# First gather ahead of the result rows, turns in place of unread products, and GpSimd making a quarter of two low parts of every item

## The reference, cut to what matters

```
logits = h @ w_router + b_router
top_val, top_idx = lax.top_k(logits, 4)
gates = softmax(top_val)
# for each expert e, over the tokens that chose it (their order is by expert):
hgu   = xs @ w_gate_up[e] + b_gate_up[e]          # 1024 -> 2048, gate and linear columns interleaved
act   = min(g,7) * sigmoid(1.702*min(g,7)) * (clip(l,-7,7) + 1)
out   = (act @ w_down[e] + b_down[e]) * gate      # 1024 -> 1024
moe   = segment_sum(out, token)
h     = layernorm(alpha * h + moe, ln2_g, ln2_b)
```

## Time and profile before

| | us |
|---|---|
| median of 3 runs | 1944.49 (1944.4 to 1946.3) |
| the profiled execution, whole | 1945.81 |
| its span | 1944.1 |
| ahead of the experts | about 690 |
| items 0 and 1 | about 757 to 830 |
| the loop of small and big items | about 830 to 1800 |
| three late items, final layernorm | about 1800 to 1944 |

### The profile page before, as it was taken

How to read it: one execution, slowest core, us unless ns; L and a number is a source line. 1 busy time by engine, 2 the same in 40 slices (tenths; PEclk the granted TensorE clock), 3 DMA queues, 4 the chain that set the end, 5 groups by cost and what they waited for, 6 DMA issues and landing times.

```text
span 1944.1 us, 28693 instructions
## 1 busy us (share of the span) xinstructions
PE 1849.6 (95%) x8487; PEld 1445.6 (74%) x8487; DVE 1665.5 (86%) x1783; ACT 1351.0 (69%) x1777; POOL 497.5 (26%) x395
## 2 busy tenths in 40 slices
PE   6999999998989997999999999999999999999887
PEld 3657767787768886877877787777778777777665
DVE  6899997448775566999999999999999999999887
ACT  4556865214346524798889888888888888888775
POOL 6671000000000114422421522423232322222121
PEclk7999999999999996999999999999999999999998
DMA  8222216332110157999999999999999999999994
GB/s 318 87 108 87 86 63 209 120 103 63 64 44 23 32 141 273 316 404 384 395 392 395 389 397 397 385 391 400 347 401 402 395 384 383 397 394 343 326 339 193
DMA packets 133073, 523.37 MB, mean 269 GB/s; under 512 B 15145, under 2 KB 20425, under 8 KB 112848
## 3 DMA queue, kind: packets, MB, share of 16 engines
q1 hardware_dynamic: 118704, 492.45, 66.5%
q0 software_dynamic: 14304, 30.11, 5.7%
HBM read 512.76 MB, written 19.29 MB: 274 GB/s over the span
## 4 chain that ended last, share of the span: by engine, by line
PE 39%; ACT 6%; DMA 6%; DVE 5%; issue 4%; ACTq 0%; SPq 0%; DVEq 0%
PE ps L1148 32%; DMA arena<-in_w_gate_up 6%; PE ps L1197 3%; DVE split L2851 3%; ACT arena_r L2046 2%; ACT split L2046 2%; ACT arena L2075 2%; PE ps L1101 1%; DVE arena_r L2851 1%; PE ps L1187 1%; DMA ring<-in_w_down 1%; DVE arena L2989 0%; DVE small L2982 0%; DVE aTs L2795 0%; SPq L675 0%
## 5 line engine op out<-in xcount | busy, mean ns | idle before, releaser
L1148 PE MATMUL ps<-split,xTs 128*128 128x512 f32 x2016 | 503.1, 397 | 8.4 <-DVE split L2851 5.4
L1148 PEld LDWEIGHTS ps<-split,xTs 128*128 128x128 f32 x2016 | 377.8, 190 | 103.8 <-DVE split L2851 19.3
L2851 DVE TENSOR_TENSOR split<-arena,split 128x2048 fp32r<-128x2048 f32 x166 | 376.9, 2284 | 11.5 <-ACT split L2046 10.6
L2046 ACT ACTIVATE split<-arena 128x1024 fp32r<-128x1024 f32 x332 | 330.1, 1052 | 28.6 <-DMA arena<-in_w_gate_up 19.2
L2851 DVE TENSOR_TENSOR split<-ring,split 128x2048 fp32r<-128x2048 f32 x106 | 241.5, 2292 | 0.0
L854 POOL DMA_INDIRECT y_rows<-arena,slots x33 | 144.8, 4389 | 305.4 <-issue 263.4
L2046 ACT ACTIVATE split<-ring 128x1024 fp32r<-128x1024 f32 x212 | 212.4, 1057 | 3.6 <-DMA ring<-in_w_gate_up 2.9
L2851 DVE TENSOR_TENSOR arena_r<-arena,arena_r 128x2048 fp32r<-128x2048 f32 x83 | 189.8, 2286 | 2.1 <-ACT arena_r L2046 2.1
L1148 PE MATMUL ps<-arena_r,xTs 128*128 128x512 f32 x672 | 180.7, 403 | 1.8 <-DVE arena_r L2851 1.6
L2046 ACT ACTIVATE arena_r<-arena 128x1024 fp32r<-128x1024 f32 x166 | 172.0, 1057 | 13.3 <-DMA arena<-in_w_gate_up 10.8
L1148 PE MATMUL ps<-arena_r,aTs 128*128 128x512 f32 x672 | 169.3, 397 | 0.0
(11 more groups left out here) (484 smaller groups left out, 3155.3 us busy)
## 6 DMA issues: line engine op xcount, KB each, us to landing
arena<-in_w_gate_up SPq DMA_DIRECT2D x170, 1024.0 KB, 13.8
ring<-in_w_gate_up SPq DMA_DIRECT2D x102, 1024.0 KB, 14.4
arena<-in_w_down SPq DMA_DIRECT2D x79, 1024.0 KB, 13.9
ring<-in_w_down SPq DMA_DIRECT2D x57, 1024.0 KB, 14.3
ring<-in_w_in SPq DMA_DIRECT2D x23, 1024.0 KB, 4.9
ring<-in_w_out SPq DMA_DIRECT2D x8, 1024.0 KB, 5.0
ring<-in_mod_w SPq DMA_DIRECT2D x10, 512.0 KB, 9.1
ring<-in_mod_w SPq DMA_DIRECT2D x4, 1024.0 KB, 4.9
```

The source lines that it names most:

```text
L1148: m = mm(ps[:, banks + q, :], lhs[:, x_, k, :], w[:, q * 512:(q + 1) * 512], start=start, stop=stop)
L2046: A(split_part(0, c), chunk(it, c), ACT.Copy).then_inc(sig("hi_ready"), 1)
L2851: V.tensor_tensor(split_pair(1, p), slot_tile(it.slot(p)), split_pair(0, p), ALU.subtract).then_inc(sig("lo_ready"), 1)
```

## The change

Five edits.

1. GpSimd gathers item 0's tokens ahead of the four `y_dram` stores, which now stand right behind that gather. The two loads of layernorm constants move behind the 16 stores of pairs, just ahead of item 1's rows.
2. SP loads item 0's tiles in the order `FIRST_LOADS`: 7 and 6 ahead of 3, 4 and 5, each at an earlier condition of its own.
3. The two bias loads count on one semaphore instead of two.
4. In small items `keep_busy(4)` is gone, and `turn_next` stands in its place, ahead of the second `turn_sum`.
5. In every item but item 0, GpSimd writes the first 512 of the 2048 columns of the low parts of pairs 6 and 8 (`pool_low`), and DVE the other 1536. PE waits for both before the low products of these pairs, ACT before it overwrites their high parts, SP before it reloads their slots. In GpSimd's order the first piece stands behind the `slot_g` load and the second behind the `slot_s` load.

The rest of the diff, cut to its core:

```
+FIRST_LOADS = (0, 1, 2, 7, 6, 3, 4, 5, 8, 9, 10, 11)
+POOL_PAIRS = (6, 8)
+POOL_WIDE = 512
+    def by_pool(self, p):
+        return self.i * len(POOL_PAIRS) + (POOL_PAIRS.index(p) + 1 - len(POOL_PAIRS))
...
-            for j in range(EXPERT_TILES):
+            for j in FIRST_LOADS:
                 if j < RING1:
                     sp.wait_ge(*last_use(max(n for n in range(N_PHASE1) if n % RING1 == j)))
+                elif j == RING1 + 4:
+                    sp.wait_ge(sig("bgu_lo"), 1)
+                elif j == RING1 + 3:
+                    sp.wait_ge(sig("o_used"), TC + 1)
                 elif j == RING1:
                     sp.wait_ge(sig("o_used"), TC + 2)
-                elif j == RING1 + 3:
-                    sp.wait_ge(sig("bgu_lo"), 1)
...
                 wait_alone(sp, sig("lo_ready"), sp.to_reg(it.pairs + (LEAD + j + 1)))
+                if it.pairs_shared and j in POOL_PAIRS:
+                    wait_alone(sp, sig("lo_pool"), sp.to_reg(it.by_pool(j)))
...
+            def pool_low(it, p):
+                c_ = slice(0, POOL_WIDE)
+                wait_alone(pool, sig("hi_ready"), pool.to_reg(it.pairs * 2 + (2 * p + 1)))
+                wait_alone(pool, sig("lo_used"), pool.to_reg(it.pairs + (p + 1)))
+                nc.gpsimd.tensor_tensor(split_pair(1, p)[:, c_], slot_tile(it.slot(p))[:, c_], split_pair(0, p)[:, c_], ALU.subtract).then_inc(sig("lo_pool"), 1)
...
                         pe.wait_ge(sig("lo_ready"), it.pairs + (LEAD + p + 1))
+                        if it.pairs_shared and p in POOL_PAIRS:
+                            pe.wait_ge(sig("lo_pool"), it.by_pool(p))
...
                         up(7)
-                        keep_busy(4)
+                        turn_next()
                         turn_sum(1)
-                        turn_next()
...
-                V.tensor_tensor(split_pair(1, p), slot_tile(it.slot(p)), split_pair(0, p), ALU.subtract).then_inc(sig("lo_ready"), 1)
+                c_ = slice(POOL_WIDE if it.pairs_shared and p in POOL_PAIRS else 0, 2 * D)
+                V.tensor_tensor(split_pair(1, p)[:, c_], slot_tile(it.slot(p))[:, c_], split_pair(0, p)[:, c_], ALU.subtract).then_inc(sig("lo_ready"), 1)
```

More of the change, by code:

```diff
@@ L116, in __init__ @@
         self.loads, self.begin = loads, begin
+        self.pairs_shared = rows is not None
+    def by_pool(self, p):
+        return self.i * len(POOL_PAIRS) + (POOL_PAIRS.index(p) + 1 - len(POOL_PAIRS))
     def slot(self, j):
@@ L793, in _ @@
             for q in range(2):
-                pool.dma_start(bgu_raw[q * E:(q + 1) * E, :], a["b_gate_up_2"][:, :]).then_inc(sig("bgu_in"), 16)
+                pool.dma_start(bgu_raw[q * E:(q + 1) * E, :], a["b_gate_up_2"][:, :]).then_inc(sig("bias_in"), 16)
             nc.gpsimd.memset(bgu_raw[2 * E:, :], 0.0).then_inc(sig("pads_zero"), 1)
@@ L807, in _ @@
                 pool.dma_start(h1_dram[t * P:(t + 1) * P, :], h1[:, t, :]).then_inc(sig("h1_stored"), 16)
-            for t in range(TC):
-                pool.dma_start(y_dram[t * P:(t + 1) * P, :], h1[:, t, :]).then_inc(sig("y_begun"), 16)
-            load_rows(ln_rows[:, 0, :], "ln2_g", D, sig("ln_rows_in"))
-            load_rows(ln_rows[:, 1, :], "ln2_b", D, sig("ln_rows_in"))
             pool.wait_ge(sig("pads_zero"), 6)
@@ L829, in _ @@
             gather(idx_first[:, 0:1])
+            for t in range(TC):
+                pool.dma_start(y_dram[t * P:(t + 1) * P, :], h1[:, t, :]).then_inc(sig("y_begun"), 16)
             pool.wait_ge(sig("oh_ready"), 1)
@@ L851, in _ @@
             store_pairs(8, TC * TOPK)
+            load_rows(ln_rows[:, 0, :], "ln2_g", D, sig("ln_rows_in"))
+            load_rows(ln_rows[:, 1, :], "ln2_b", D, sig("ln_rows_in"))
             def scatter(n):
@@ L878, in item_rows @@
                     load_slots(slot_g, m + 2, P, sig("slot_g_in"))
+                pool_low(it, POOL_PAIRS[0])
                 wait_alone(pool, sig("scattered"), pool.to_reg(m * 16))
                 load_slots(slot_s, m, HALF_SLOTS if it.small else P, sig("slot_s_in"))
+                pool_low(it, POOL_PAIRS[1])
                 wait_alone(pool, sig("hi_used"), pool.to_reg(it.pairs * 2 + (SPLITS + (15 if it.small else 11))))
@@ L2004, in _ @@
                 mix_high(i)
-            act.wait_ge(sig("bgu_in"), 32)
+            act.wait_ge(sig("bias_in"), 80)
             act.wait_ge(sig("pads_zero"), 5)
             A(bgu[:], bgu_raw, ACT.Copy).then_inc(sig("bgu_hi"), 1)
-            act.wait_ge(sig("bias_in"), 48)
             A(bdown, bdown_raw, ACT.Copy).then_inc(sig("bgu_hi"), 1)
@@ L2045, in split_high_of @@
                         act.wait_ge(sig("lo_ready"), it.pairs + (c // 2 + 1))
+                        if it.pairs_shared and c // 2 - LEAD in POOL_PAIRS:
+                            act.wait_ge(sig("lo_pool"), it.by_pool(c // 2 - LEAD))
                     A(split_part(0, c), chunk(it, c), ACT.Copy).then_inc(sig("hi_ready"), 1)
```

## The result

The changed kernel took 1964.78 us (median of 4 runs, 1962.56 to 1970.87) against 1945.17 us for the kernel before (4 runs): a ratio of 1.0098, interval [1.0081, 1.0116]. It is **slower by 19.6 us**, where 2.8 us less was forecast and 1957 was the end of the range. The profiled execution took 1962.57 us, with a span of 1960.9.

What follows compares the result with a forecast made beforehand. Engines were taken to bound the early loop, memory the later part. Terms -12.9 + 12.6 + 1.8 + 2.7 - 7.0 = -2.8 us took the median from 1944.5 to 1941.7 us, range 1930 to 1957.

Steps and rivals of the forecast that it cites:

- The front: Ahead of item 0, PE's 9.84 us wait for the first gather goes and its clock stays up: -12.9 us.
- the clock: In item 0, PE's transposes and first products run faster if PE doesn't stop: 3.1 us more come off.
- Turns: In small items, transposes replace unread products; PE reaches down(10) 0.80 us sooner but waits there: 0 us.
- The piece in item 1: In up(6) of item 1, PE stalls 8.6 us for GpSimd's piece, plus constants and lost clock: +12.6 us.
- Pieces in the loop: In 14 pairs of items, GpSimd's pieces cost DVE about 0.2 us per small item: +1.8 us in sum.
- The port rival: In small items, the second piece starts ahead of DVE's low part 7 and delays it 1.06 us: +16, 1958; chance 0.15.
- One late small item: In one small item after late items are counted, a late list load makes PE wait for the piece: +2.7 us.
- Memory: In the loop's second half, weights loaded ahead during item 1's stall recover most of 8.3 us lost: -7.0 us.
- The rival of the lost lead (3): In item 1's stall the load queue runs dry and the second half still loses its 8 us: 1949; chance 0.12.
- Rival (1): Early PE time counts in small items, or item 1's piece comes before PE wants it: 1929; chance 0.23.
- (4): At the front, weights hold up the gather, which lands no sooner; 9.8 to 12.9 us come back: 1953; chance 0.05.

Runs made afterwards that it cites:

- edits 1 to 3: The kernel before with only the first three edits, turns and low parts as before: 1946.6 us, ratio 1.0001 to the kernel before.
- edit 4 alone: The kernel before with only the next item's transposes in place of the 4 unread products: 1945.9 us, ratio 0.9998 to the kernel before.
- the early piece: The changed kernel with GpSimd's piece of pair 6 ahead of the first list load in every item: 1955.3 us, ratio 1.0044 to the kernel before.

## Why the prediction was wrong

Three terms of the sum failed: the front, the late small items, and the memory. The first is the largest and an error of mechanism.

**The front, -12.9: the step that failed first.** The 9.84 us wait went, as forecast. Of the 3.1 us for the clock (the rows cited give 2.7) only the 0.8 of the transposes came, and "PE needs pair 2 at about 754, so it hides" was wrong: the y stores landed at 757 and not 751, for I priced them at 400 GB/s by themselves and overlooked the two tiles that SP issues beside them (held back, they let the stores land at 748.75). The engines kept 3.5 to 7.3 us of it, depending on the memory (table, edits 1 to 3). And the sum took it as gained at the end, where it was 0.0 (1.0001, 2.6 us either way): ACT's waits for tiles in the first half of the loop rose from 6.3 to 19.8 us instead. I had seen that the landing times rise until the memory sets the pace, and used this only for the stall; by the same argument a gain ahead of a stage that the memory limits is worth little at the end.

**Turns, 0: right** for edit 4 alone, with the wait named (1.31 us for 1.2).

**The piece in item 1, +12.6: right in kind and nearly in size.** The wait was 8.72 for 8.6 us. By the traces the piece lengthened the way into the loop by 10.2 us (109.9 against 99.7) and 10.7 (113.6 against 102.9), where 12.6 was summed.

**Pieces in the loop, +1.8: about right.** Ordinary pairs took 66.6 to 66.95 us for 66.57, so the bound of 1.1 a pair wasn't touched. The port rival did not occur in this order; with the early piece it did, at another place than I had put it (the activation's last step, not low part 7), at 0.8 to 0.9 us a pair.

**One late small item, +2.7: mis-sized, 12.4 us.** Two items were late, not one, at 5.7 and 6.7 us over a pair's 66.57. I took the lateness of the list load from the trace of before as given. But the small operations that make it late are themselves held by DVE's subtractions, and GpSimd's chain is longer once it carries pieces: in the first of the two 1 us from the pieces, 6 us from nine small operations. Each wait then cost the clock as well (12 products in 4.56 us, 2.92 before).

**Memory, -7.0: failed.** The lead did appear (landing times of 8.2 us at 960 to 1025 and 10.8 at 830 to 890), and the pairs from 1469 to 1669 were back at 66.6 us. But the seven pairs lost 1.4 us instead of gaining 7, since the two pairs at the late list's stores took 7.9 us more than 2 x 66.57, where they had taken 4.3 more; the other five gained 2.2 us. Why the dip cost more here stays open, as its depth does. I had put those 4.3 us of the kernel before down to the general pace, without looking at the stretch in which they lay.

In the table's terms (one execution each): into the loop +7.0 where -0.3 was summed, the first half +13.3 for +3.6, the second +1.4 for -6.1, the end -2.9 for 0. The rival of the lost lead (3) was nearest to what the second half did; for its sum it took the front as gained. It wasn't right either: its number was 1949. Rival (1) fell with the turns and with the wait in item 1, and (4) since the gather landed in time. The mechanism that decided the sign beside it, pieces late behind GpSimd's own blocks, stood in the text as a single item and in no rival.

## What to carry to other kernels

Before adding up gains of engines ahead of a long loop, ask what the loop's last stage waits for: if transfers set its pace, a gain upstream only spends their lead, and taking 4% of the bytes away tells it in one run. Work given to an engine that mostly waits inherits every wait ahead of it in that engine's order, and comes late exactly where that order is longest; look for the longest item, not the usual one. When a wait for a transfer is removed, the next transfer of the same queue is the first candidate for the new wait.

## What the runs showed of the chip that I had not expected

- Over the 10 us behind 64 pieces of 4 bytes the 16 DMA engines stood at a busy share of 0.94 and 145 GB/s, where 400 is usual here; 32 pieces of 8 bytes left 280. By the difference to 400 I estimate that the first cost the weights about 6 us of their time, the second 3.
- Eight operations of 128x32 on GpSimd took 4.52 us in one trace and 8.47 in the other, with the same instructions: single ones went from 0.28 to 2.1 to 2.3 us when they met a subtraction of DVE.
- Two engines sharing one subtraction, three quarters and one quarter, made the larger part take 2.35 us on the mean of 66, longer than the whole alone (2.28).
